# Two transformer blocks on one core: the front of the next block scaled inside its transposes, and four weight units of it split ahead into places of their own

## The chip, the core and the metric

The kernel runs on one core of a Trainium2 chip. The core has a matrix engine (TensorE, PE), a vector engine (VectorE, DVE), an activation engine (ScalarE, ACT), GpSimd (POOL) and SyncE (SP). Each has its own queue of instructions, and they wait for each other on semaphores. Data comes from HBM by DMA; here SP issues the loads of weights, POOL those of the conditioning matrix. The metric is device microseconds of one execution.

## What is computed

Two blocks on a sequence of 256 tokens with model width 2048, all in fp32:

```
def first_block(x, ...):
    h = rmsnorm(x, g_pre)
    o, z = swa_sink_mixer(h, w_in_a, sinks_a)
    y = (o * silu(z)) @ w_out_a
    return x + rmsnorm(y, g_post)

def second_block(x, c, ...):
    mod = silu(c) @ w_ada + b_ada
    sh1, sc1, gt1, sh2, sc2, gt2 = split(mod, 6)
    h = rmsnorm(x, g_pre_mix) * (1 + sc1) + sh1
    proj = h @ w_in
    ...                     # two attentions, gated, then @ w_o
    x = x + gt1 * rmsnorm(y, g_post_mix)
    h = rmsnorm(x, g_pre_ffn) * (1 + sc2) + sh2
    f = square(relu(h @ w_ff1)) @ w_ff2
    return x + gt2 * rmsnorm(f, g_post_ffn)
```

There are two places where a norm of a sum just made feeds the next product: `x` of the first block into `w_in` (called change 1), and `x` behind `w_o` into `w_ff1` (change 2).

## The kernel before

**Units and turns.** Weights go through the core in units of 128 x 1024 (two k tiles of 128 x 512, 512 KB). Eight units (`UPT`) are a turn: one product of all 16 k tiles with 512 columns of weights, for two tiles of 128 tokens. There are 76 turns. A unit is used in three fp32r products per k tile and token tile, `three` (L1751 to L1753): high part of h by high part of w, high by low, low by high; 12 products a unit. SP loads the unit into `raw` (4 slots), ACT rounds it into `w_hi` (L677), DVE subtracts into `w_lo` (L1109), both three units ahead of PE (`AHEAD`). A load waits for the low part of the unit four before, ACT's rounding for PE's products of the unit four before. The semaphores `hi_ready`, `lo_ready` and `mm_done` count these steps, and each engine does its steps in the order in which its function writes them; nothing else sets the order.

**The last turn before a change** (turn 12 before change 1, turn 43 before change 2) is `residual_turn`. PE does units 0 to 3 as usual, then units 4 to 7 for token tile 0 and only then for tile 1, so that the norm of tile 0 runs beside tile 1's products. DVE splits on to unit 7 (at change 1 with four products of conditioning, `ada_first`, between, and `make_mod`, which puts together the scale `pre_gain` and shift `pre_shift`, one column for each k tile). Behind the last products ACT squares the result (`square_y`), DVE scales it by the gain (`scale_y`) and adds it to x (`add_residual`, L1170), ACT squares x (`norm_squares`, L681) and takes roots, and DVE writes a diagonal matrix of 1/rms for each token tile (`diagonal_of`, L1210).

**The first turn behind it** (13 and 44) is `norm_turn`. PE transposes x, a k tile at a time (`norm_turned`, L1797), as soon as x is there, multiplies all ones by the diagonals into a bank, so that 1/rms stands in every row (L1826), and ACT copies that row (`norm_row`, L700). DVE then scales each transposed tile by gain and row (`norm_scale`, L1231), ACT adds the shift and rounds to `h_hi` (`norm_hi`, L707), DVE makes `h_lo` (`norm_lo`, L1238), two k tiles a unit. Unit 0 starts when the first k tile's `h_lo` is there (`front_unit`). Where PE has nothing to do it multiplies ones by the identity into an unused bank (`idle_at_change`, L1816), 12, 6 and 11 times (`IDLE_AT`).

**Conditioning.** The products of `silu(c)` with `w_ada` are done by DVE, one per 128 x 1024 (`ada_first`, L1114), between its other work; POOL loads their matrices into four buffers, each load behind the product that used the buffer before. `ADA_OUT` says at which units of turns 9 to 11 they stand. Later ones are for the gates and use two of the buffers.

## Time and profile before

| | |
|---|---|
| median of 3 runs | 1751.14 us (1750.18 to 1752.04) |
| profiled execution | 1750.48 us, its span 1748.8 us |
| PE busy with products | 1735.9 us, 99% of the span |
| DVE, ACT, POOL busy | 72%, 50%, 13% |
| DMA, mean | 264 GB/s |

The profile is of one execution. The page lists busy times, the chain of work that ended last and the costliest groups; the timeline lists instructions in order of time, counted from the span's start, and merges like ones that follow each other (x2). A record's time is from start to end, and records overlap in an engine's pipeline, so the step between starts can be less than the duration. An fp32 product that is no transpose shows as two records on PE. In brackets stands how long the engine was idle before, and what released it.

### The profile page before, as it was taken

To read this page: it belongs to the slowest core of one execution; us is meant where nothing else is said; L and a number is where in the kernel's file an instruction comes from. 1 tells how busy PE (TensorE), PEld (TensorE's weight loads), DVE (VectorE), ACT (ScalarE), POOL (GpSimd) and SP (SyncE) were. 2 spreads that over 40 slices of the span, in tenths; PEclk is the share of its full clock that TensorE was granted. 3 is DMA by queue.
4 is the path that set the end of the run, shared out by engine and by line. 5 is a ranking of instruction groups with operands and counts; after the bars stand their busy time and mean duration, and the time that the engine had idled before them with its cause. 6 is when DMAs were issued, how large, how long until landed. Compare 5 with 4: busy or idle time off the path is not lost.

```text
span 1748.8 us, 24683 instructions
## 1 busy us (share of the span) xinstructions
PE 1735.9 (99%) x8030; PEld 1433.7 (82%) x8030; DVE 1260.5 (72%) x1876; ACT 870.5 (50%) x1197; POOL 224.8 (13%) x446
## 2 busy tenths in 40 slices
PE   9999999999999999999999999999999999999998
PEld 7778878887888888888888888888888888888886
DVE  5798879868988788677678778777765555555555
ACT  6866674544445444444445455444444444444444
POOL 0232402001144233200001100000000000000000
PEclk9999999999999999999999999999999999999999
DMA  9899879554789888898998957999988765555553
GB/s 344 280 345 327 301 259 388 217 173 150 261 254 306 278 272 281 306 304 285 327 314 299 322 173 248 306 324 316 306 287 266 241 218 193 193 193 194 193 193 136
DMA packets 145663, 462.18 MB, mean 264 GB/s; under 512 B 21920, under 2 KB 33840, under 8 KB 144832
## 3 DMA queue, kind: packets, MB, share of 16 engines
q1 hardware_dynamic: 109200, 344.46, 58.6%
q0 software_dynamic: 36256, 116.91, 19.3%
q8 instruction: 33, 0.54, 0.1%
q14 instruction: 30, 0.25, 0.0%
q10 hardware_dynamic: 144, 0.02, 0.0%
HBM read 437.18 MB, written 12.08 MB: 257 GB/s over the span
## 4 chain that ended last, share of the span: by engine, by line
PE 94%; DVE 3%; ACT 2%; issue 1%; DMA 0%; SPq 0%; DVEq 0%; ACTq 0%
PE bank L1751 30%; PE bank L1752 30%; PE bank L1753 30%; PE bank L1788 1%; DVE w_lo L1109 0%; ACT w_hi L677 0%; PE bank L2028 0%; PE bank L2037 0%; DVE x L1170 0%; DMA raw<-in_w_in_a 0%; ACT y L681 0%; PE bank L1816 0%; PE bank L1906 0%; DVE ada_raw L1114 0%; DVE ada_more L1114 0%
## 5 line engine op out<-in xcount | busy, mean ns | idle before, releaser
L1109 DVE TENSOR_TENSOR w_lo<-raw,w_hi 128x1024 fp32r<-128x1024 f32 x605 | 728.5, 1210 | 433.3 <-ACT w_hi L677 429.2
L677 ACT ACTIVATE w_hi<-raw 128x1024 fp32r<-128x1024 f32 x605 | 633.8, 1050 | 736.8 <-PE bank L1753 666.2
L1751 PE MATMUL bank<-w_hi,h_hi 128*128 128x512 f32 x2272 | 889.5, 391 | 2.7 <-DVE w_lo L1253 1.2
L1752 PE MATMUL bank<-w_lo,h_hi 128*128 128x512 f32 x2272 | 884.3, 389 | 0.0
L1753 PE MATMUL bank<-w_hi,h_lo 128*128 128x512 f32 x2272 | 884.3, 389 | 0.0
L1751 PEld LDWEIGHTS bank<-w_hi,h_hi 128*128 128x128 f32 x2272 | 426.5, 188 | 96.3 <-issue 6.4
L1753 PEld LDWEIGHTS bank<-w_hi,h_lo 128*128 128x128 f32 x2272 | 426.4, 188 | 89.2
L1752 PEld LDWEIGHTS bank<-w_lo,h_hi 128*128 128x128 f32 x2272 | 426.6, 188 | 86.7
L1114 DVE CUSTOM_DVE_ANT_0 ada_raw<-ada_raw,cond 128x1024 f32<-128x1024 f32 x160 | 194.5, 1217 | 9.2 <-DMA ada_raw<-in_w_ada 9.2
L549 POOL DMA_DIRECT2D ada_raw<-in_w_ada x160 | 85.4, 534 | 784.8 <-DVE loop_sums L1114 586.4
L402 POOL DMA_DIRECT2D rope_ab<-rot x96 | 47.1, 499 | 142.7 <-DVE rot L1454 141.9
L405 POOL DMA_DIRECT2D p_back<-post_gain x100 | 49.0, 499 | 32.8 <-ACT post_gain L827 20.6
L1751 PE MATMUL bank<-w_hi,o_hi 128*128 128x512 f32 x128 | 49.8, 389 | 0.0
L1752 PE MATMUL bank<-w_lo,o_hi 128*128 128x512 f32 x128 | 49.8, 389 | 0.0
L1753 PE MATMUL bank<-w_hi,o_lo 128*128 128x512 f32 x128 | 49.8, 389 | 0.0
L1114 DVE CUSTOM_DVE_ANT_0 ada_more<-ada_more,cond 128x1024 f32<-128x1024 f32 x32 | 38.5, 1218 | 0.0
L1751 PEld LDWEIGHTS bank<-w_hi,o_hi 128*128 128x128 f32 x128 | 24.0, 188 | 5.0
L1063 ACT ACTIVATE f_buf<-bank 128x512 f32<-128x512 f32 x32 | 19.2, 600 | 17.9 <-PE bank L1753 17.9
L1752 PEld LDWEIGHTS bank<-w_lo,o_hi 128*128 128x128 f32 x128 | 24.0, 188 | 5.0
L1753 PEld LDWEIGHTS bank<-w_hi,o_lo 128*128 128x128 f32 x128 | 24.0, 188 | 5.0
L549 POOL DMA_DIRECT2D ada_more<-in_w_ada x32 | 17.0, 531 | 54.6 <-DVE loop_sums L1114 24.1
L1691 DVE STREAM_TRANSPOSE f_buf<-f_buf 128x512 f32<-128x512 f32 x32 | 22.8, 711 | 1.1
(240 smaller groups left out, 867.4 us busy)
## 6 DMA issues: line engine op xcount, KB each, us to landing
raw<-in_w_ff SPq DMA_DIRECT2D x256, 512.0 KB, 4.6
raw<-in_w_in SPq DMA_DIRECT2D x176, 512.0 KB, 5.0
ada_raw<-in_w_ada POOLq DMA_DIRECT2D x160, 512.0 KB, 6.2
raw<-in_w_in_a SPq DMA_DIRECT2D x69, 512.0 KB, 6.2
ada_more<-in_w_ada POOLq DMA_DIRECT2D x32, 512.0 KB, 6.2
raw<-in_w_out_a SPq DMA_DIRECT2D x32, 512.0 KB, 6.5
raw<-in_w_o SPq DMA_DIRECT2D x32, 512.0 KB, 5.2
raw<-in_w_moba SPq DMA_DIRECT2D x16, 512.0 KB, 5.6
```

Of the source, the lines that this page charges most:

```text
L402: eng.dma_start(rope_ab[j * QUAD:(j + 1) * QUAD, i * T * P:(i + 1) * T * P], rot_flat[i * QUAD:(i + 1) * QUAD, j * T * P:(j + 1) * T * P]) ...
L405: eng.dma_start(back[j * QUAD:(j + 1) * QUAD, i * MASK_W:(i + 1) * MASK_W], blocks[i * QUAD:(i + 1) * QUAD, j * MASK_W:(j + 1) * MASK_W]). ...
L549: pool.dma_start(two(ada_slot(slot), 1), w_ad[:, bass.ds((k + part * KT) * 2 + half, 1), :])\
L677: act.activation(used(w_hi, turn, s), used(raw, turn, s), ACT.Copy).then_inc(hi_ready, 1)
L1063: act.activation(f_tok[:, t, :], pair[p][t][:, :], ACT.Relu).then_inc(evicted[p][t], 1)
L1109: dve.tensor_tensor(used(w_lo, turn, s), used(raw, turn, s), used(w_hi, turn, s).bitcast(F32), ALU.subtract).then_inc(lo_ready, 1)
L1114: dve.tensor_tensor_reduce(w, w, cond[:, half * (D // 2):(half + 1) * (D // 2)], 1.0, 0.0, ALU.mult, ALU.add, dst).then_inc(ada_done, 1)
L1691: dve.transpose(by_quadrant[:, t], f_tok[:, t, :]).then_inc(f_blocked, 1)
L1751: pe.matmul(out_ap, hi, rhs_hi, start=start, stop=False)
L1752: pe.matmul(out_ap, hi, rhs_lo, start=False, stop=False)
L1753: return pe.matmul(out_ap, lo, rhs_hi, start=False, stop=stop)
L1788: ins = pe.transpose(dst[:, b * P:(b + 1) * P], src[:, t, b * P:(b + 1) * P], ident)
```

## The change

The first two k tiles are no longer transposed and then scaled. PE multiplies them by the diagonal of 1/rms (`front_turn`), which turns and scales in one, into two banks of their own (`front_bank`); ACT applies `pre_gain` and `pre_shift` and rounds straight from the bank (`front_hi`), and DVE makes the low part in two steps, bank times gain minus high, then plus shift (`front_lo`). The row of 1/rms is still made for the other k tiles. PE's fill products go from 12, 6 and 11 to 12, 4 and none.

Units 0 to 3 of the turn behind the change get buffers of their own (`ext_raw`, `ext_hi`, `ext_lo`, the low part over the raw one), loaded, rounded and subtracted in the last turn before the change, each behind a unit of that turn. Units 4 to 7 are loaded into the usual slots and split in the turn itself (`NEXT_SPLITS`). The four conditioning products that stood in turn 12 stand now at units 0 to 3 of turn 9, and the others keep their units. Space for that comes from moving the scratch `sq1`, `sq2` into `f_buf`. The diff, without the buffers' places and the counts of semaphores:

```diff
...
+        sq1 = sq2 = f_buf[:, 3 * CH:4 * CH]
...
-        ADA_OUT = (range(4, 8), range(0, 8), range(0, 8))
+        ADA_OUT = (range(0, 8), range(0, 8), range(0, 8))
...
-        IDLE_AT = (12, 6, 11)
+        IDLE_AT = (12, 4)
+        def front_bank(k):
+            return pair[PAIR_B][1] if k else banks[SCORES]
...
+        NEXT_SPLITS = {0: 4, 1: 5, 2: 6, 3: 7, 5: 8, 6: 9, 7: 10}
...
+            def load_ext(r, s, src):
+                if s == 0 and r == 1:
+                    sp.wait_ge(og_ready, T * (CHUNKS + 1))
+                if s == 0 and r == 2:
+                    sp.wait_ge(mm_done, TURN_WO * UPT)
+                    sp.wait_ge(h_lo_ready, H_WO + UPT)
+                sp.dma_start(two(ext_raw[r][:, s, :], 1), src).then_inc(ext_loaded[s], 16)
+            def load_last(r, turn, w, c, w_next, c_next):
+                for s in range(UPT):
+                    load(turn, s, unit_at(w, c, s))
+                    if s < EXT:
+                        load_ext(r, s, unit_at(w_next, c_next, s))
+                for s in range(EXT, UPT):
+                    load(turn + 1, s, unit_at(w_next, c_next, s))
...
-            with sp.Fori(0, CHUNKS) as i:
+            with sp.Fori(0, CHUNKS - 1) as i:
                 load_chunk(i + TURN_OUT, w_oa, i)
-            load_chunk(TURN_QI, w_2, CHUNK_QI)
+            load_last(1, TURN_QI - 1, w_oa, CHUNKS - 1, w_2, CHUNK_QI)
...
-            with sp.Fori(0, D // CH) as i:
+            with sp.Fori(0, D // CH - 1) as i:
                 load_chunk(i + TURN_WO, w_oo, i)
+            load_last(2, TURN_FF1 - 1, w_oo, CHUNKS - 1, w_f1, 0)
...
                 pool.dma_start(x[:, t, :], x_in[t * P:(t + 1) * P, :]).then_inc(x_again, 16)
+            for n in range(UPT // 2):
+                load_first(40, n, SC1, 14)
             pool.wait_ge(o1_ready, (CHUNKS - 1) * PAIRS_A + 2)
             load_gain(0, g_post)
-            for n in range(UPT // 2):
-                load_first(40, n, SC1, 14)
             for n in range(2 * UPT):
...
                 act.activation(used(w_hi, turn, s), used(raw, turn, s), ACT.Copy).then_inc(hi_ready, 1)
+            def split_ext(r, turn, s):
+                act.wait_ge(ext_loaded[s], 16 * r)
+                if s == 0 and r == 1:
+                    act.wait_ge(h_lo_ready, H_OUT + UPT)
+                if s == 0 and r == 2:
+                    act.wait_ge(mm_done, TURN_WO * UPT)
+                act.activation(ext_hi[r][:, s, :], ext_raw[r][:, s, :], ACT.Copy).then_inc(hi_ready, 1)
+            def split_next(turn, s):
+                act.wait_ge(raw_loaded[s % SLOTS], (turn * (UPT // SLOTS) + s // SLOTS + 1) * 16)
+                act.wait_ge(mm_done, unit_of(turn - 1, s) + 1)
+                act.activation(used(w_hi, turn, s), used(raw, turn, s), ACT.Copy).then_inc(hi_ready, 1)
...
+            def front_hi(r):
+                act.wait_ge(mod_ready, r)
+                for k in range(KG):
+                    act.wait_ge(front_turned, KG * (r - 1) + k + 1)
+                    act.activation(h_hi[:, k, :], front_bank(k)[:, 0:SEQ], ACT.Identity, bias=pre_shift[:, k:k + 1],
+                                   scale=pre_gain[:, k:k + 1]).then_inc(n_rounded, 1)
...
             def norm_turn(r, turn):
-                for s in range(2):
-                    norm_hi(r, s)
-                split(turn, 2)
-                for s in range(UPT):
-                    split(turn, s + AHEAD)
+                norm_hi(r, 1)
+                for s in range(UPT):
+                    if s in NEXT_SPLITS:
+                        (split_next if s < EXT else split)(turn, NEXT_SPLITS[s])
                     if s + 2 < UPT:
...
                     split(turn, s + AHEAD)
+                    if s:
+                        act.sem_inc(raw_loaded[s - 1], 16)
+                    if s < EXT:
+                        split_ext(r, turn, s)
                 for t in range(T):
...
                     y_roots(r, t, n + t + 1)
-                    if t == 0:
-                        split(turn, UPT)
-                    else:
+                    if t:
                         front_root(r)
-                        split(turn, UPT + 1)
                     norm_squares(r, t, y)
                 back_root(r)
+                front_hi(r)
                 norm_row(r)
...
                                   ALU.subtract).then_inc(lo_ready, 1)
+            def split_last(turn, s):
+                dve.wait_ge(hi_ready, count_last(turn, s))
+                dve.tensor_tensor(w_lo[:, s % SLOTS, :], raw[:, s % SLOTS, :], w_hi[:, s % SLOTS, :].bitcast(F32),
+                                  ALU.subtract).then_inc(lo_ready, 1)
+            def split_ext(r, turn, s):
+                dve.wait_ge(hi_ready, count_ext(turn, s))
+                dve.tensor_tensor(ext_lo[r][:, s, :], ext_raw[r][:, s, :], ext_hi[r][:, s, :].bitcast(F32),
+                                  ALU.subtract).then_inc(lo_ready, 1)
...
                 for s in range(TILE_FROM + 1):
-                    split(turn, s + AHEAD)
-                    if r == 1 and s < TILE_FROM:
-                        ada_first(60, s, mod_column(SC1, s // 2, s % 2))
+                    split_last(turn, s + AHEAD)
+                    if s < EXT:
+                        split_ext(r, turn, s)
                     if s == TILE_FROM - 1:
...
                     add_residual(r, t, y)
-                    if t == 0:
-                        split(turn, UPT)
                 back_stats(r)
-                split(turn, UPT + 1)
                 dve.wait_ge(mod_ready, r)
                 norm_first(r, pre_gain)
-                split(turn, UPT + 2)
...
+            def front_lo(r, gain):
+                for k in range(KG):
+                    rest = norm_tmp[:, 0, k * SEQ:(k + 1) * SEQ]
+                    dve.wait_ge(n_rounded, KT * r + k + 1)
+                    dve.scalar_tensor_tensor(rest, front_bank(k)[:, 0:SEQ], gain[:, k:k + 1], h_hi[:, k, :].bitcast(F32),
+                                             ALU.mult, ALU.subtract).then_inc(n_scaled, 1)
+                    dve.wait_ge(n_scaled, KT * (r - 1) + k + 1)
+                    dve.tensor_scalar(h_lo[:, k, :], rest, pre_shift[:, k:k + 1], None, ALU.add)\
+                        .then_inc(h_lo_ready if k else h_front_ready, 1)
...
             def norm_first(r, gain):
-                norm_scale(r, 0, gain)
-                norm_lo(r, 0)
+                front_lo(r, gain)
                 norm_scale(r, 1, gain)
...
                 for s in range(UPT):
-                    split(turn, s + AHEAD)
+                    if s in NEXT_SPLITS:
+                        split(turn, NEXT_SPLITS[s])
                     if s + 2 < UPT:
...
+            def ext_unit(r, turn, s, p, h):
+                pe.wait_ge(h_lo_ready, h + s + 1)
+                pe.wait_ge(lo_ready, count_ext(turn - 1, s))
+                for t in range(T):
+                    mm = unit_tile(s, t, h_hi, h_lo, KG * s, p, False, False, w_at=(ext_hi[r][:, s, :], ext_lo[r][:, s, :]))
+                mm.then_inc(mm_done, 1)
+            def front_turn(r, t, k):
+                pe.wait_ge(x_stat, X_STATS[r] + (8 if t else 4))
+                pe.wait_ge(x_new, ((r - 1) * T + t) * CHUNKS + 1)
+                return pe.matmul(front_bank(k)[:, t * P:(t + 1) * P], x[:, t, k * P:(k + 1) * P], rstd_diag[:, t, :],
+                                 start=True, stop=True)
             def idle_at_change(r, n):
...
                 idle_at_change(r, IDLE_AT[0])
-                for s in range(ahead):
+                for s in range(1, ahead):
                     norm_turned(r, s)
                 idle_at_change(r, IDLE_AT[1])
-                pe.wait_ge(x_stat, X_STATS[r] + 7)
+                for k in range(KG):
+                    front_turn(r, 0, k)
+                for k in range(KG):
+                    front_turn(r, 1, k).then_inc(front_turned, 1)
                 for t in range(T):
...
                 ins.then_inc(rstd_spread, 1)
-                idle_at_change(r, IDLE_AT[2])
-                for s in range(UPT):
-                    if s:
+                for s in range(UPT):
+                    if s == 0:
+                        front_unit(r, turn, p, use, h)
+                    elif s < EXT:
+                        ext_unit(r, turn, s, p, h)
+                    else:
                         chunk_unit(turn, s, p, use, h)
-                    else:
-                        front_unit(r, turn, p, use, h)
                     if s in (0, 2):
...
                             norm_turned(r, turned)
```

On PE, from the last product of turn 12 to unit 0 of turn 13 (`consts` holds ones and identity, `norm_rows` the diagonals). Before:

```order
L1753 MATMUL bank<-w_hi,h_lo 128x512
L1816 MATMUL bank<-consts 128x128 x12
L1797 MATMUL bank<-consts,x 128x128 x16
L1816 MATMUL bank<-consts 128x128 x6
L1826 MATMUL bank<-norm_rows,consts 128x128 x2
L1816 MATMUL bank<-consts 128x128 x11
L1751 MATMUL bank<-w_hi,h_hi 128x512
```

The same place after:

```order
L1819 MATMUL bank<-w_hi,h_lo 128x512
L1894 MATMUL bank<-consts 128x128 x12
L1864 MATMUL bank<-consts,x 128x128 x12
L1894 MATMUL bank<-consts 128x128 x4
L1890 MATMUL bank<-norm_rows,x 128x128 x4
L1907 MATMUL bank<-norm_rows,consts 128x128 x2
L1817 MATMUL bank<-ext_hi,h_hi 128x512
```

Four transposes have become four products with the diagonals, ahead of the spreading of the row, and nothing stands between that and unit 0 any more.

On DVE, from tile 1's root to the low parts of unit 1 (`post_gain` holds the scaled tiles). Before:

```order
L1208 RECIPROCAL x_rstd<-x_rstd 128x1
L1210 TENSOR_SCALAR norm_rows<-consts,x_rstd 128x128
L1109 TENSOR_TENSOR w_lo<-raw,w_hi 128x1024
L1231 SCALAR_TENSOR_TENSOR post_gain<-bank,pre_gain,norm_rows 128x256 x2
L1238 SCALAR_TENSOR_TENSOR h_lo<-post_gain,pre_shift,h_hi 128x256 x2
L1231 SCALAR_TENSOR_TENSOR post_gain<-bank,pre_gain,norm_rows 128x256 x2
```

The same place after:

```order
L1265 RECIPROCAL x_rstd<-x_rstd 128x1
L1267 TENSOR_SCALAR norm_rows<-consts,x_rstd 128x128
L1302 SCALAR_TENSOR_TENSOR post_gain<-bank,pre_gain,h_hi 128x256
L1305 TENSOR_SCALAR h_lo<-post_gain,pre_shift 128x256
L1302 SCALAR_TENSOR_TENSOR post_gain<-bank,pre_gain,h_hi 128x256
L1305 TENSOR_SCALAR h_lo<-post_gain,pre_shift 128x256
L1288 SCALAR_TENSOR_TENSOR post_gain<-bank,pre_gain,norm_rows 128x256 x2
```

The split of a weight unit is gone from there, and the front's k tiles take turns instead of going in pairs.

On DVE in turn 12, from unit 6's low part to unit 7's (the five short ones are `make_mod`). Before, with a product of conditioning behind unit 6:

```order
L1109 TENSOR_TENSOR w_lo<-raw,w_hi 128x1024
L1114 ISA ada_more,mod_part<-ada_more,cond 128x1024
L1114 ISA mod_part 128x1
L1130 TENSOR_TENSOR pre_gain<-mod_part 128x16
L1132 TENSOR_TENSOR pre_gain<-pre_gain,mods 128x16
```

The same place after:

```order
L1166 TENSOR_TENSOR w_lo<-raw,w_hi 128x1024
L1170 TENSOR_TENSOR ext_lo<-ext_raw,ext_hi 128x1024
L1191 TENSOR_TENSOR pre_gain<-mod_part 128x16
L1193 TENSOR_TENSOR pre_gain<-pre_gain,mods 128x16
```

An early split of the next turn's unit stands where the product stood; so it is behind units 3, 4 and 5 too.

## Rows read from the trace of the kernel before

**Rows 1.** The page, the chain that ended last, by line of the kernel.
```profile
PE bank L1751 30%; PE bank L1752 30%; PE bank L1753 30%; PE bank L1788 1%; DVE w_lo L1109 0%; ACT w_hi L677 0%; PE bank L2028 0%; PE bank L2037 0%; DVE x L1170 0%; DMA raw<-in_w_in_a 0%; ACT y L681 0%; PE bank L1816 0%; PE bank L1906 0%; DVE ada_raw L1114 0%; DVE ada_more L1114 0%
```

**Rows 2.** Timeline, change 1: start us, us, engine, line, operation [idle before].
```profile
330.49 0.39 PE L1753 MATMUL bank<-w_hi,h_lo 128*128 128x512 f32 x1
...
333.35 0.63 ACT L681 ACTIVATE y<-x 128x512 f32<-128x512 f32 x1 [0.32 <-DVE x L1170]
...
336.48 0.16 DVE L1208 RECIPROCAL x_rstd<-x_rstd 128x1 f32<-128x1 f32 x1 [0.53 <-ACT x_rstd L696]
...
336.67 0.29 DVE L1210 TENSOR_SCALAR norm_rows<-consts,x_rstd 128x128 f32<-128x128 f32 x1
...
337.01 0.71 PE L1826 MATMUL bank<-norm_rows,consts 128*128 128x128 f32 x4 [0.34 <-DVE norm_rows L1210]
...
337.56 2.62 PE L1816 MATMUL bank<-consts 128*128 128x128 f32 x22
...
337.76 0.38 ACT L700 ACTIVATE norm_rows<-bank 128x256 f32<-128x256 f32 x1 [1.32 <-PE bank L1826]
...
338.28 0.88 DVE L1231 SCALAR_TENSOR_TENSOR post_gain<-bank,pre_gain,norm_rows 128x256 f32<-128x256 f32 x2 [0.18 <-ACT norm_rows L700]
...
338.86 0.91 ACT L707 ACTIVATE h_hi<-post_gain,pre_shift 128x256 fp32r<-128x256 f32 x2 [0.71 <-DVE post_gain L1231]
...
339.40 0.89 DVE L1238 SCALAR_TENSOR_TENSOR h_lo<-post_gain,pre_shift,h_hi 128x256 fp32r<-128x256 f32 x2 [0.24 <-ACT h_hi L707]
...
340.03 0.47 PE L1751 MATMUL bank<-w_hi,h_hi 128*128 128x512 f32 x1
```

**Rows 3.** Timeline, change 2: last product before it, first behind it.
```profile
1032.84 0.39 PE L1753 MATMUL bank<-w_hi,h_lo 128*128 128x512 f32 x1
...
1042.44 0.47 PE L1751 MATMUL bank<-w_hi,h_hi 128*128 128x512 f32 x1
```

**Rows 4.** Groups by line and shape: count, busy us, mean ns, idle before.
```profile
L1529 DVE TENSOR_SCALAR post_gain<-s,l_inv 128x256 f32<-128x256 f32 x16 | 5.6, 348 | 0.0
```

**Rows 5.** Windows: us, PE, PEld, DVE, ACT, POOL busy, PEclk, DMA share, GB/s.
```profile
248.00:259.00 11.00, 11.00 (x64) 8.45 (x63) 5.58 (x10) 6.72 (x12) 0.00 (x0) 1.00 0.44 147
...
292.00:303.00 11.00, 11.00 (x50) 9.13 (x49) 9.90 (x13) 4.25 (x4) 2.61 (x5) 1.00 1.02 412
...
340.00:351.00 11.00, 11.00 (x58) 9.28 (x57) 10.81 (x21) 8.28 (x13) 0.00 (x0) 1.00 0.38 129
```

**Rows 6.** Timeline, turn 9: DVE's gating and low parts, PE's unit 6.
```profile
257.03 1.29 DVE L1344 TENSOR_TENSOR o_gated_t<-bank,o_t 128x512 f32<-128x512 f32 x2 [1.01 <-PE bank L1788]
...
259.02 1.30 DVE L1275 TENSOR_TENSOR h_lo<-o_gated_t,h_hi 128x512 fp32r<-128x512 f32 x2 [0.70 <-ACT h_hi L763]
...
259.97 0.39 PE L1751 MATMUL bank<-w_hi,h_hi 128*128 128x512 f32 x1
```

**Rows 7.** DMA issues, that of 292.98 alone: KB, us to landing.
```profile
raw<-in_w_out_a SPq DMA_DIRECT2D x1, 512.0 KB, 6.7
```

**Rows 8.** Timeline, end of turn 12: DVE, then PE's first product of unit 7.
```profile
318.47 1.23 DVE L1109 TENSOR_TENSOR w_lo<-raw,w_hi 128x1024 fp32r<-128x1024 f32 x1 [0.35 <-ACT w_hi L677]
...
319.61 1.22 DVE L1114 CUSTOM_DVE_ANT_0 ada_more<-ada_more,cond 128x1024 f32<-128x1024 f32 x1
...
320.94 0.17 DVE L1130 TENSOR_TENSOR pre_gain<-mod_part 128x16 f32<-128x16 f32 x1
...
321.75 1.22 DVE L1109 TENSOR_TENSOR w_lo<-raw,w_hi 128x1024 fp32r<-128x1024 f32 x1
...
323.92 0.39 PE L1751 MATMUL bank<-w_hi,h_hi 128*128 128x512 f32 x1
```

**Rows 9.** Windows, columns as in rows 5: loads ahead of change 2.
```profile
1000.00:1011.00 11.00, 11.00 (x50) 9.13 (x49) 8.50 (x11) 4.93 (x6) 1.58 (x3) 1.00 0.89 298
```

**Rows 10.** Timeline at the start; a window behind the last product.
```profile
1.21 4.90 PE L1840 MATMUL bank<-s 128*128 128x128 f32 x22 [1.21 <-POOL s L581]
...
1743.30:1748.00 4.70, 0.00 (x0) 0.00 (x0) 2.52 (x4) 0.00 (x0) 0.00 (x0) 0.50 0.62 223
```

59 lines of the change are left out of this document (38 added, 21 removed).

## Prediction

> **What bounds the kernel now.** I read the page first: TensorE (PE) carries 94% of the chain that ended last, and 90% of the span are the products of weight units, three lines of 30% each [rows 1]. So the time changes only where PE stands still, does work that is no product, or would come to stand still. The changed code touches two stretches, the changes between blocks, so I read the timeline there. At change 1 the last product before it starts at 330.49 and the first after it at 340.03 [rows 2]; at change 2 these are 1032.84 and 1042.44 [rows 3]. In between PE does transposes and products of constants that nobody reads. What really ends the stretch is a chain through four engines: square of the last result, scaling by the gain, square root, four residual additions, their squares, a root, the diagonal of 1/rms written by VectorE (DVE) at 336.67 for 0.29 us; then PE spreads it over all rows (337.01), ScalarE (ACT) copies the row (337.76), DVE scales the transposed tiles (338.28), ACT rounds and shifts (338.86), DVE makes the low part (339.40), PE begins (340.03) [rows 2]. From the diagonal's arrival on PE to the first product that is 3.02 us. Change 2 shows the same durations 702.4 us later [rows 3], so what is worked out for one counts twice.
>
> **Part 1, the shorter chain (a gain).** Everything up to 337.01 stays: the same operations in the same order; the splits of weights taken out there (one on ACT, one on DVE) stood beside waits: ACT sat idle for 0.32 us before its squares of the second half, until DVE's addition released them [rows 2]. After 337.01 the row copy and one DVE pass go. New chain: two PE records per fp32 product. The first of a batch takes 0.38 and four take 0.71 with steps of 0.11 behind the first step [rows 2], so two take 0.71-0.22 = 0.49. Then ACT, scaling and shifting out of the bank: between 0.38, its copy out of a bank of the same size [rows 2], and 0.50, its shift of 128x256 (two in 0.91, 0.41 apart); I take 0.50, since scale and shift are the latter's kind. DVE's product-minus-high from the bank: 0.48 (two in 0.88, 0.40 apart) [rows 2]. DVE's add of the shift, 128x256 from SBUF: between 0.35, a tensor_scalar of that size [rows 4], and the same 0.48; I take 0.35. Hops between steps are 0.03 (DVE to itself, 336.64 to 336.67), 0.05 (DVE to PE, 336.96 to 337.01) and 0.14 (ACT to DVE, 338.14 to 338.28) [rows 2]; I take 0.2 for all four. Sum 0.49+0.50+0.48+0.35+0.2 = 2.02; against 3.02 that gains 1.0. With 0.48 for the add and hops of 0.15 it is 2.45, a gain of 0.55. I take 0.95 per change, 1.9 in all.
>
> The second half of the first unit waits for the other tile's low part. On DVE that is 0.48+0.35 plus hops behind the first, 0.9 us, while PE has 6 products of 0.23 = 1.4 us to do, so it costs nothing. Unit 1 then needs scaling, rounding and low part of its two tiles; for unit 0 these took 338.28 to 340.29, 2.0 us [rows 2]. From DVE's end with the front at 339.8 that gives 341.8, while PE has unit 0 (12 products, 2.7 us) and eight transposes (1.0 us) to do from 339.1 and comes at 342.8. Nothing is late behind.
>
> **Part 2, four units split ahead.** In the stretch behind the change PE had no gap to give back, busy 11.00 of 11 us, with DVE at 10.81 and ACT at 8.28 [rows 5]. So early splits gain nothing there. Their work is the same count of splits (1.06 on ACT, 1.22 on DVE, where the next starts after 1.14 [rows 8]) moved into the last turn before a change, where PE takes 2.72 per unit and the two splits need 2.1 and 2.3: they fit if data is there. The four conditioning products (1.22 each) that stood there at change 1 go to the start of turn 9.
>
> **Part 3, their new place (nothing, up to 1).** In turn 9 they stand with the attention of the last heads. DVE is busy only 5.58 of 11 us at 248 to 259 [rows 5]. In its order the last of the four stands ahead of a split of weights that ended 1.0 us before the gating which reads PE's transposes (idle 1.01, start 257.03) [rows 6]. One product of 1.14 us (DVE's step) more ahead of it makes the gating 0.1 late; the other three stand further ahead, in idle time. Behind it hangs the low part of the unit that PE begins at 259.97; it is ready at 259.02+0.65 = 259.67 [rows 6]. 0.3 us of slack takes that. I count 0; if the products fall badly, up to one of them, 1.2.
>
> **Part 4, the transfers (a cost at change 1).** SP now issues an extra 512 KB behind each of the first four loads of turn 12, issued at 293 to 301. There the DMA engines are already full, at 412 GB/s and a share of 1.02 [rows 5], and a load lands 6.7 us after its issue [rows 7]. At 0.412 MB/us one load of 0.524 MB takes 1.27 us alone and 2.53 beside POOL's. Unit 0 of turn 12 lands at 299.7 (issued 292.98). Up to unit 4 there now come 8 loads instead of 4. POOL's last conditioning load is issued where DVE's fourth product of turn 11 ends, at about 299.4, and lands at about 307; until then 7.3/2.53 = 2.9 loads get through; the other 5.1 take 6.5 us, to 313.5. The four loads that POOL issued behind it are gone, but its next two, for the gate, wait only for the count of finished products, which is now reached at about 308 and 312; they take about one load's time from SP's queue, 1.4 us. So unit 4 lands at about 314.9. From there ACT and DVE have a full row: high part 1.06, six low parts at steps of 1.14 (units 4 to 6 and three extras), the modulation vectors 0.81 (320.94 to 321.75) and the low part of unit 7, 1.22: 9.96 with the hop, done at 324.9. PE begins the products of unit 7 at 323.92, and had its low part at 322.97 [rows 8]. That is a stall of 1.0 us, and each us of the landing is one of the stall. The bounds: all eight loads at the full rate, 299.7+10.2 = 309.9, no stall; all at half, 299.7+20.2 = 319.9, a stall of 6.0.
>
> Those two rates are the row's total and its half. On who gets which share the Trainium skill (DMA: Bandwidth & Descriptors, Queues, rings and completion order) says that an engine takes turns between the queues that have work, packet by packet. By that rule SP's queue has half as long as POOL's has work, and the stall stays at about 1.0; were SP's queue served first it would be none.
>
> At change 2 the same extra loads meet less, 298 GB/s [rows 9]. Four of them in about 9 us add 0.23 MB/us, which makes 0.53 against 0.412, 1 MB too much by their end or 2.5 us of delay. Change 1 had 1.0 us between low part and need although its loads landed 2 us later after issue, so I count 0, at most 0.5.
>
> **Sum.** Against the profiled execution: -1.9 for the two chains, +1.0 for the late unit at change 1: -0.9, 1750.48 to 1749.6. That execution lies 0.7 under the median of the runs shown, so against it 1751.14-0.9 = 1750.2.
>
> **Rivals.** (a) No stall: the queue drains in time. For it: only 1 us separates landing and need. Time 1751.14-1.9 = 1749.2. (b) The extra loads stay at half rate, because POOL's gate loads come early and the products' loads stretch: PE stands up to 6.0 us at unit 7 of turn 12. This alone ends slower than before: it does from a landing of unit 4 at 315.9 on, and at 319.9 gives 1751.14-1.9+6.0 = 1755.2. Against it: POOL's queue is empty for some time after 307. (c) The clock. PE loses 13 of 29 fill products per change, and stands still some 0.5 us before the diagonal and 0.6 us before the first product. The trace shows 22 records of 128x128 in 4.90 us at the start [rows 10] against 22 in 2.62 us at change 1 [rows 2]: the lower level (1.2 GHz) at first, 2.4 GHz later; the granted clock is 1.00 in every window of the changes [rows 5] and 0.50 only behind the last product, where PE does nothing [rows 10]. If each change brings the lower level for as long as the start had it, 4.9 us, half is lost: 2.4 per change, 1751.14-1.9+4.8 = 1754.0. The rows speak against it: the new order stands still for less than 1 us at a time, and only behind the last product has standing still cost the level.
>
> The Trainium skill (TensorE: Matmul & The Clock Gate, What's actually happening) has the gate follow how busy PE was lately, which speaks against removing fill work; how much is enough no row here shows, so (c) keeps a small chance.
>
> (d) The chain is not shortened at all, because something beside it is late (a turned tile, a bank): 0 or a little more, 1751.1 to 1752. (e) More than both chains comes back; nothing in the rows offers it.
>
> **Chances.** Forecast (stall 0.2 to 2.0) 43%; (a) 30%; (b) beyond 2.0 10%; (c) 5%; (d) 6%; (e) 6%. About 0.2% (3.5 us, 1747.6 to 1754.6) is what a measurement of this kernel can tell from no change. Faster than that: (e) and 2% of (a), 8%. Slower: the far part of (b), and (c) where it comes with the stall, 8%. The rest, 84%, is within. The range: the low end is (a) with both gains at 1.0 and the spread of the runs, 1751.14-2.0-1.0 = 1748.1; the high end takes in (d) and most of (b), 1753.0.
>
> **What would show it.** The first product after change 1 should start about 2.0 us after PE's product with the diagonal starts, and likewise at change 2. Loads of units 1 to 4 of turn 12 should take 9 to 11 us to land instead of 7; DVE's low part of unit 7 should end about 1 us later against PE's products, with a gap on PE before the products of that unit. The clock row should stay at 1.00. The forecast is wrong if the chain from diagonal to product is above 2.5 us, or if PE shows gaps of more than 2 us anywhere in turns 9 to 12.

## The result, and the profile after

| | before | after |
|---|---|---|
| median of 20 runs | 1750.84 us (1749.90 to 1752.04) | 1753.53 us (1750.35 to 1755.56) |
| profiled execution | 1750.48 us, span 1748.8 | 1751.51 us, span 1749.8 |

The ratio is 1.0014, interval 1.0008 to 1.0020: 2.7 us slower, where the prediction had 1750.2 and a range up to 1753.0. The runs after also scatter more, 5.2 us from lowest to highest instead of 2.1, and the profiled execution is one of the quick ones. So one trace can't hold the whole answer.

PE after the change, from the late part of turn 12 to the first product behind change 1 (columns as in rows 2):

```profile
323.06 0.50 PE L1817 MATMUL bank<-w_hi,h_hi 128*128 128x512 f32 x1 [0.61 <-DVE w_lo L1166]
...
324.32 0.40 PE L1819 MATMUL bank<-w_hi,h_lo 128*128 128x512 f32 x1
326.14 0.50 PE L1817 MATMUL bank<-w_hi,h_hi 128*128 128x512 f32 x1 [1.42 <-DVE w_lo L1166]
326.48 0.39 PE L1818 MATMUL bank<-w_lo,h_hi 128*128 128x512 f32 x1
...
332.85 0.39 PE L1819 MATMUL bank<-w_hi,h_lo 128*128 128x512 f32 x1
333.08 2.84 PE L1894 MATMUL bank<-consts 128*128 128x128 f32 x24
335.75 1.73 PE L1864 MATMUL bank<-consts,x 128*128 128x128 f32 x12
337.32 1.06 PE L1894 MATMUL bank<-consts 128*128 128x128 f32 x8
338.21 0.61 PE L1890 MATMUL bank<-norm_rows,x 128*128 128x128 f32 x4
339.38 0.71 PE L1890 MATMUL bank<-norm_rows,x 128*128 128x128 f32 x4 [0.55 <-DVE norm_rows L1267]
339.92 0.61 PE L1907 MATMUL bank<-norm_rows,consts 128*128 128x128 f32 x4
341.65 0.47 PE L1817 MATMUL bank<-ext_hi,h_hi 128*128 128x512 f32 x1 [1.12 <-DVE h_lo L1305]
```

Against [rows 2], the last product to the first behind it is 332.85 to 341.65, 8.80 us instead of 9.54. The gain of the chain is there. But ahead of it stand two new waits, 0.61 before unit 6 and 1.42 before unit 7 of turn 12, where PE ran through before. Each costs some 0.3 us more than the idle time in brackets: products start 0.23 apart when nothing holds them up, but from 324.32 to 326.14 it is 1.82, and 0.34 more to the next.

What those waits hang on is the row of splits on DVE; the same trace:

```profile
315.62 1.22 DVE L1170 TENSOR_TENSOR ext_lo<-ext_raw,ext_hi 128x1024 fp32r<-128x1024 f32 x1
317.25 1.23 DVE L1166 TENSOR_TENSOR w_lo<-raw,w_hi 128x1024 fp32r<-128x1024 f32 x1 [0.41 <-ACT w_hi L714]
...
321.80 1.22 DVE L1166 TENSOR_TENSOR w_lo<-raw,w_hi 128x1024 fp32r<-128x1024 f32 x1
322.93 1.22 DVE L1170 TENSOR_TENSOR ext_lo<-ext_raw,ext_hi 128x1024 fp32r<-128x1024 f32 x1
324.07 0.17 DVE L1191 TENSOR_TENSOR pre_gain<-mod_part 128x16 f32<-128x16 f32 x1
...
324.87 1.22 DVE L1166 TENSOR_TENSOR w_lo<-raw,w_hi 128x1024 fp32r<-128x1024 f32 x1
```

From unit 4 (317.25) to unit 7 (its low part ends at 326.09) DVE never waits for data. It started late because ACT did, and ACT waited for the load of unit 4:

```profile
316.15 1.06 ACT L714 ACTIVATE w_hi<-raw 128x1024 fp32r<-128x1024 f32 x1 [1.67 <-DMA raw<-in_w_out_a]
```

That load was issued at 303.09 and took 13.0 us to land; before, unit 4's took 7.0, and that of unit 0, in [rows 7], 6.7:

```profile
raw<-in_w_out_a SPq DMA_DIRECT2D x1, 512.0 KB, 13.0
```

The windows (columns as in rows 5) show where the DMA engines' time was full: from 292 to 314 the share is 1.00 and 1.03, and the window behind that, with 0.65, is the first in which PE is not busy all the time.

```profile
292.00:303.00 11.00, 11.00 (x51) 9.09 (x50) 10.38 (x14) 4.25 (x4) 2.65 (x5) 1.00 1.00 399
303.00:314.00 11.00, 11.00 (x50) 9.13 (x49) 6.66 (x11) 4.92 (x8) 0.86 (x2) 1.00 1.03 412
314.00:325.00 11.00, 10.11 (x44) 7.59 (x42) 10.49 (x15) 7.23 (x8) 0.20 (x1) 1.00 0.65 242
```

The kernel before had the same full engines up to 314, with nothing late, so a full share alone doesn't tell of a stall; its windows from 303 on:

```profile
303.00:314.00 11.00, 11.00 (x50) 9.09 (x50) 10.30 (x15) 5.52 (x8) 2.12 (x4) 1.00 1.03 415
314.00:325.00 11.00, 11.00 (x50) 9.13 (x49) 8.82 (x19) 3.18 (x3) 1.06 (x2) 1.00 0.90 312
```

**Cutting the span.** Since executions scatter by more than the effects, I cut each trace at five starts on PE: the first product of probabilities with values in turn 4 (L1906 before, L1988 after), the first fill behind turn 12, the first product behind change 1, the first fill and the first product at change 2; "rest" ends where PE's last product starts. "Change 1" and "change 2" in the table are the stretches from first fill to first product. Such a stretch repeats to about 0.1 us when nothing disturbs it. The start of the kernel does not: the first cut lies anywhere from 100.33 to 103.26 in these traces, with code there that is the same.

| kernel | first cut | to change 1 | change 1 | to change 2 | change 2 | rest | this execution |
|---|---|---|---|---|---|---|---|
| before | 101.01 | 229.71 | 9.31 | 693.04 | 9.37 | 698.03 | 1750.48 |
| after | 100.68 | 232.40 | 8.57 | 693.25 | 8.62 | 698.00 | 1751.51 |

So the change costs 2.69 ahead of change 1, and gains 0.74 and 0.75 at the two changes; the start was 0.33 earlier by chance. That explains 1751.5, but not the median of 1753.5, 1.3 above what these parts give (1750.84+2.69-1.49+0.2 = 1752.2).

### The profile page after: what moved, and what is told of

Read it like the earlier page. It is cut to its first block, busy times and chain, and to the rows that moved or that the text cites. A ratio compares the mean times of both kernels' runs of the same rounds, so it can differ in the third digit from the quotient of the medians.

```text
span 1749.8 us, 24558 instructions
## 1 busy us (share of the span) xinstructions
PE 1732.1 (99%) x7986; PEld 1428.9 (82%) x7986; DVE 1260.5 (72%) x1876; ACT 869.4 (50%) x1197; POOL 225.5 (13%) x446
## 4 chain that ended last, share of the span: by engine, by line
PE 92%; DVE 3%; ACT 2%; DMA 1%; issue 1%; SPq 0%; DVEq 0%; ACTq 0%
PE bank L1817 30%; PE bank L1819 29%; PE bank L1818 29%; DMA raw<-in_w_out_a 1%; ACT w_hi L714 1%; PE bank L1855 1%; DVE w_lo L1162 1%; PE bank L2110 0%; PE bank L2119 0%; DVE x L1231 0%; ACT y L729 0%; DMA raw<-in_w_in_a 0%; PE bank L1988 0%; DVE ada_raw L1175 0%; DVE ada_more L1175 0%
## 5 line engine op out<-in xcount | busy, mean ns | idle before, releaser
L1162 DVE TENSOR_TENSOR w_lo<-raw,w_hi 128x1024 fp32r<-128x1024 f32 (+1 forms) x587 | 707.0, 1210 | 430.0 <-ACT w_hi L714 426.1
L714 ACT ACTIVATE w_hi<-raw 128x1024 fp32r<-128x1024 f32 x589 | 617.2, 1050 | 732.9 <-PE bank L1819 638.8
L1817 PE MATMUL bank<-w_hi,h_hi 128*128 128x512 f32 x2240 | 876.9, 391 | 4.9 <-DVE w_lo L1166 2.0
L1818 PE MATMUL bank<-w_lo,h_hi 128*128 128x512 f32 x2240 | 871.9, 389 | 0.0
L1819 PE MATMUL bank<-w_hi,h_lo 128*128 128x512 f32 x2240 | 871.8, 389 | 0.0
L1817 PEld LDWEIGHTS bank<-w_hi,h_hi 128*128 128x128 f32 x2240 | 420.6, 188 | 97.5 <-issue 6.2
L1819 PEld LDWEIGHTS bank<-w_hi,h_lo 128*128 128x128 f32 x2240 | 420.5, 188 | 88.0
L1818 PEld LDWEIGHTS bank<-w_lo,h_hi 128*128 128x128 f32 x2240 | 420.7, 188 | 85.8
```

Source lines behind the costliest of these rows:

```text
L714: act.activation(used(w_hi, turn, s), used(raw, turn, s), ACT.Copy).then_inc(hi_ready, 1)
L1162: dve.tensor_tensor(used(w_lo, turn, s), used(raw, turn, s), used(w_hi, turn, s).bitcast(F32), ALU.subtract).then_inc(lo_ready, 1)
L1817: pe.matmul(out_ap, hi, rhs_hi, start=start, stop=False)
L1818: pe.matmul(out_ap, hi, rhs_lo, start=False, stop=False)
L1819: return pe.matmul(out_ap, lo, rhs_hi, start=False, stop=stop)
```

## The experiments

All are timed beside runs of the kernel before. The intervals of a ratio with 11 runs are 0.0009 to either side, or 1.6 us, so the medians alone settle few of the questions. The stretches of the table tell more, but each is of one profiled execution.

### Taking the change apart

**chain_only**: the kernel before with the scaled transposes alone.

```diff
-                norm_scale(r, 0, gain)
-                norm_lo(r, 0)
+                front_lo(r, gain)
...
-                for s in range(2):
-                    norm_hi(r, s)
+                norm_hi(r, 1)
...
                 back_root(r)
+                front_hi(r)
                 norm_row(r)
...
-        IDLE_AT = (12, 6, 11)
+        IDLE_AT = (12, 4)
```

> The kernel before with Part 1 alone: the front scaled inside its transposes, all splits, loads and conditioning where they were. Theory (transfers): the extra time of the changed kernel comes from its loads in turn 12, none from the new chain; its profile gives 2.27 us from PE's product with the second diagonal to the first product instead of 3.02, so each change should gain 0.75 us and the time fall by 1.5, from 1750.8 to 1749.3, with runs as close together as those of the kernel before (some 2 us from lowest to highest). Rival (chain): the new order on PE and ACT is what costs or scatters; then this kernel is at 1751 or above, and its runs spread over 4 us or more.

Measured 1749.59 (1749.07 to 1752.90) beside 1750.92; ratio 0.9993, 0.9984 to 1.0002. To change 1 it takes 229.75, as before, and the changes 8.57 and 8.63. Nine runs lie within 1 us, two at 1752.80 and 1752.90. The second is the profiled one, and it has a late start (103.26) and a wait of 1.11 us just before 948, for DVE's `y_tok`, far from what was changed; the clock is at 1.00. The first has a mean granted clock of 0.997, the lowest of the eleven, as a fall of the clock would leave it; the others have 0.998 and 0.999. So the median is as the theory had it and the scatter is not. The gain of the chain is seen in the stretches and is all there without the rest; the interval of the ratio alone still holds 1.

**ext_only**: the changed kernel with the old chain.

```diff
-                front_lo(r, gain)
+                norm_scale(r, 0, gain)
+                norm_lo(r, 0)
...
-        IDLE_AT = (12, 4)
+        IDLE_AT = (12, 6, 11)
```

> The changed kernel with the old chain put back: the early splits, their loads and the move of the conditioning products stay. Theory (transfers): PE again stands before units 6 and 7 of turn 12, 2 us in a good run and more in others; without the 1.5 us of the two chains the median is 1753.5+1.5 = 1755.0, and the runs spread over 4 us or more. Rival (chain): 1750.8 to 1751.5, close together.

Measured 1754.10 (1752.08 to 1754.79); ratio 1.0017, 1.0008 to 1.0026. Gaps of 0.60 and 1.41 before units 6 and 7, 232.77 to change 1, and 9.31 and 9.37 at the changes. The early splits with their loads cost 3.1 us, all of it ahead of change 1.

**cond_only**: the kernel before with the four conditioning products moved to turn 9.

```diff
-        ADA_OUT = (range(4, 8), range(0, 8), range(0, 8))
+        ADA_OUT = (range(0, 8), range(0, 8), range(0, 8))
...
-                    if r == 1 and s < TILE_FROM:
-                        ada_first(60, s, mod_column(SC1, s // 2, s % 2))
```

> The kernel before with only the four conditioning products moved from turn 12 to turn 9. Theory (transfers): nothing, 1750.8 within 0.4; in the changed kernel the trace shows no gap of PE in turn 9. Rival (conditioning): the products hold up the gating of turn 9 or their loads push those of weights, by up to 1.2 us in one run and more in others; then 1752 or above.

Measured 1750.95 (1750.14 to 1752.13); ratio 0.9999, 0.9990 to 1.0008. Behind the start, all stretches are as before to 0.04 us, 229.71 to change 1 among them. The move costs nothing.

### Work or transfers

**thin_ext**: hardly any bytes, same splits. The extra loads bring 16 of 1024 columns, the early splits read the unit before (so the product behind each change is another), and the load of unit 7 waits for one more low part, since that slot is now read once more.

```diff
-                sp.dma_start(two(ext_raw[r][:, s, :], 1), src).then_inc(ext_loaded[s], 16)
+                sp.dma_start(two(ext_raw[r][:, s, 0:16], 1), src[:, :, 0:16]).then_inc(ext_loaded[s], 16)
...
+                    if s == UPT - 1:
+                        sp.wait_ge(lo_ready, unit_of(turn, s) - SLOTS + 2)
...
-                act.activation(ext_hi[r][:, s, :], ext_raw[r][:, s, :], ACT.Copy).then_inc(hi_ready, 1)
+                act.activation(ext_hi[r][:, s, :], raw[:, (s + AHEAD) % SLOTS, :], ACT.Copy).then_inc(hi_ready, 1)
```

> The changed kernel with the extra loads cut to 16 of their 1024 columns. The early splits stay, on ACT and DVE, in their places and of full size, but they read the unit split just before, so what the next turn multiplies by is not its weights. Theory (transfers): 4 MB less go through the queues ahead of the changes, the gaps of turn 12 go, and the time is 1749.4, as with the shorter chains alone. Rival (work): the extra split of each engine per unit is what makes unit 6 and 7 late; then the gaps stay and the time is 1752 or more.

229.69 to change 1, with no gap of PE in turn 12. So the stall is the loads' alone, and the splits fit into turn 12, as the prediction had it. But the median was 1750.72 (1748.75 to 1754.06) instead of 1749.4, and the profile shows one reason. PE behind change 1 in thin_ext:

```profile
339.62 0.72 PE L1819 MATMUL bank<-ext_hi,h_hi 128*128 128x512 f32 x1 [1.12 <-DVE h_lo L1307]
340.14 0.63 PE L1820 MATMUL bank<-ext_lo,h_hi 128*128 128x512 f32 x1
340.57 0.63 PE L1821 MATMUL bank<-ext_hi,h_lo 128*128 128x512 f32 x1
...
343.11 0.39 PE L1821 MATMUL bank<-ext_hi,h_lo 128*128 128x512 f32 x1
```

Its window there, with the granted clock in the third column from the end:

```profile
339.00:343.00 4.00, 3.38 (x8) 2.74 (x9) 3.75 (x11) 2.54 (x6) 0.00 (x0) 0.58 0.00 0
```

The products step by 0.43 us, not 0.23, for 3.4 us: the lower level of 1.2 GHz, and 1.6 us lost (694.80 to change 2 instead of 693.2). It came with the first product, behind 0.55 and 1.12 us of standing still. This is rival (c), which had 5%.

**late_ext**: the extra loads in the order in which the units are split.

```diff
                     load(turn, s, unit_at(w, c, s))
-                    if s < EXT:
-                        load_ext(r, s, unit_at(w_next, c_next, s))
+                    if s >= AHEAD and s < AHEAD + EXT:
+                        load_ext(r, s - AHEAD, unit_at(w_next, c_next, s - AHEAD))
```

> The changed kernel with another order of SP's loads alone: each extra load stands three places later, behind units 3 to 6 of the last turn, in the order in which the units are split. Theory (transfers): five loads fewer stand ahead of what is wanted first, unit 4 lands before 312 instead of at 316.1, the gaps before units 6 and 7 go, and the time is that of the shorter chains alone, 1749.3, runs within 2 us. Rival (work): in turn 12 ACT and DVE have an extra split per unit and can't keep up whatever the loads do; then the gaps stay, and the time is 1753 as for the changed kernel.

Measured 1751.76 (1749.77 to 1753.81), between the 1749.3 and the 1753 of the two theories; ratio 1.0005, 0.9996 to 1.0014. Unit 4 lands at 313.17, and it takes 231.26 to change 1: 1.1 us less than in the changed kernel's profile, but not all of the stall. One gap of 1.22 is left before unit 7. What ends last there is the last extra unit, which lands at 322.10; ACT waits for it, and the low part of unit 7 stands behind its low part and the modulation vectors in DVE's order:

```profile
322.12 1.06 ACT L721 ACTIVATE ext_hi<-ext_raw 128x1024 fp32r<-128x1024 f32 x1 [0.19 <-DMA ext_raw<-in_w_in]
...
323.21 1.23 DVE L1170 TENSOR_TENSOR ext_lo<-ext_raw,ext_hi 128x1024 fp32r<-128x1024 f32 x1
```

The bytes are the same, and moving them back only moves what is late.

**gate_late**: POOL's two gate loads held back.

```diff
+            pool.wait_ge(mm_done, TURN_QI * UPT)
             for n in range(2):
                 load_gate(ADA_FIRST, n, 0)
```

> The changed kernel with POOL's two loads for the gate, issued at 309.6 and 313.7 in turn 12, held back until the last product of turn 12; they are not needed before turn 16. Theory (transfers, all streams count alike): 1 MB less competes with units 4 to 7, which land 1.3 to 2.5 us earlier; 2.7 us of loss in turns 9 to 12 become 0.2 to 1.4, and the time falls to between 1750.5 and 1752.0. Rival (backlog from turn 11): only what is issued before 301 counts, and the time stays at 1753.

Measured 1752.83 (1751.41 to 1754.76); ratio 1.0011, 1.0002 to 1.0020. The 1750.5 to 1752.0 expected is missed. The gaps are 0.61 and 1.42 as ever, and it takes 232.68. Units 4 to 7 do land quicker (12.0, 8.2, 5.3 and 3.1 us after issue instead of 13.0, 9.3, 7.5 and 5.6), but DVE was busy without a break from unit 2 on, and unit 2 had waited for its load, issued before any gate load:

```profile
311.33 1.06 ACT L715 ACTIVATE w_hi<-raw 128x1024 fp32r<-128x1024 f32 x1 [3.10 <-DMA raw<-in_w_out_a]
```

In the changed kernel's profile DVE's break before unit 4 is 0.41 us, so that is about all that an earlier landing of unit 4 alone can give (an estimate): the landing of unit 2 binds next, and the gate loads come too late to touch it. The landing of unit 4 here:

```profile
raw<-in_w_out_a SPq DMA_DIRECT2D x1, 512.0 KB, 12.0
```

This trace also has a gap of 1.07 before unit 7 of turn 43, and 694.63 to change 2: the stall that the prediction excluded at change 2.

**late_both**: the two edits above together.

> Both remedies in one: the extra loads three places later in SP's queue, and POOL's two gate loads held back until the end of turn 12. The first alone left 1.55 us of loss up to the last product of turn 12 and a time of 1751.8. Theory (transfers, all streams count alike): 1 MB less is worth 1.3 to 2.5 us of landing, the rest of the stall goes, and the time is that of the shorter chains alone, 1749.4. Rival (work): what is left in turn 12 is the extra splits; the time stays at 1751.8.

229.73 to change 1: the stall is gone, and the same edits with fill (late_both_fill below) have 229.75. The two together did what neither did alone: with the extra loads further back, the loads that come last are those beside which the gate loads ran. Median 1750.23 (1748.86 to 1752.16); ratio 0.9996, 0.9987 to 1.0005. Unit 4 landed in

```profile
raw<-in_w_out_a SPq DMA_DIRECT2D x1, 512.0 KB, 7.8
```

Its profiled execution, 1752.16, had the clock at 0.50 for 3.4 us behind change 2 (699.59 in the rest instead of 698.0).

### What the slower runs lose

**after2**: the changed kernel once more.

> The changed kernel once more, beside the others of this group. In its profile so far PE stood 0.61 and 1.42 us before units 6 and 7 of turn 12, and from the first mixing products of turn 4 to the last product of turn 12 it took 2.7 us more than before; the two shorter chains give back 1.5, which makes 1.2 over the kernel before, or 1752.1. Its median was 1753.5. Theory (transfers): most runs have a longer stall than the profiled one, so a second profile may show more than 2.0 us of gaps there. Rival: the rest lies elsewhere, and the gaps of turn 12 are as they were.

Median 1753.43 (1750.78 to 1754.86), ratio 1.0011, 1.0002 to 1.0021; again a quick execution was profiled, with 232.46 to change 1, gaps of 0.62 and 1.41, and nothing else. The gaps are as they were; whether the slower runs have a longer stall stays open here.

**after_fill**: fill products in both gaps of each change. chain_fill, late_both_fill, late2_fill and thin_fill have the same edit.

```diff
-        IDLE_AT = (12, 4)
+        IDLE_AT = (12, 4, 2, 4)
...
+            def fill_at_front(p, use, n):
+                pe.wait_ge(evicted[p][1], use)
+                for _ in range(n):
+                    pe.matmul(pair[p][1][:, 0:P], ones, ident, start=True, stop=True)
...
                 for k in range(KG):
                     front_turn(r, 0, k)
+                fill_at_front(p, use, IDLE_AT[2])
                 for k in range(KG):
                     front_turn(r, 1, k).then_inc(front_turned, 1)
...
                 ins.then_inc(rstd_spread, 1)
+                fill_at_front(p, use, IDLE_AT[3])
```

> The changed kernel with six fill products back at each change, where PE stood still: two before the products with the second diagonal (a gap of 0.55 us) and four before the first weight product (a gap of 1.12 us), at 0.24 us each. One profile of a related kernel showed the granted clock at 0.50 for 3.4 us from the first product behind change 1 on, and one behind change 2; that costs 1.6 us each time. Theory (clock): most runs of the changed kernel lose the clock at one of the changes, which is the 1.3 us that its median of 1753.4 lies above what its profiled runs explain (1752.1); with the fill it is at 1752.1, and the clock stays at 1.00. Rival (stall at change 2): fill changes nothing, 1753.4.

> The shorter chain alone, which was at 1749.6 with 2 of 11 runs at 1752.8, with the same six fill products at each change. Theory (clock): where PE stands still for 0.55 and 1.12 us the clock may fall; with the fill no run does it, the median is 1749.4 and no run lies above 1751.5. Rival: the two runs at 1752.8 come from the start of the kernel and a gap of 1.1 us at 947 as the profiled one did; then some of these lie at 1752.8 too, and the median is the same.

> The changed kernel with all remedies: extra loads three places later, gate loads held back, six fill products at each change. Without the fill it was at 1750.2, and its profiled run lost 1.6 us at change 2 with the clock. Theory (clock): 1749.5, as the shorter chain alone, and the clock stays at 1.00. Rival: 1750.2 as before, the rest being a stall that comes in some runs.

| | without fill | with fill |
|---|---|---|
| changed kernel | 1753.43 (1750.78 to 1754.86) | 1752.44 (1750.94 to 1753.14) |
| chain alone | 1749.59 (1749.07 to 1752.90) | 1749.78 (1748.62 to 1751.12) |
| late_both | 1750.23 (1748.86 to 1752.16) | 1749.55 (1748.19 to 1750.93) |

The highest run falls in all three. But the two columns come from different sessions, beside medians of the kernel before of 1750.92 to 1751.05, and each difference lies within the interval of 1.6 us; the kernel before itself had single runs up to 1755.35. So the table points to the clock and doesn't show it. PE at change 1 in chain_fill; the first product still starts 2.28 us behind the product with the second diagonal, so the fill delays nothing:

```profile
335.62 0.61 PE L1838 MATMUL bank<-consts 128*128 128x128 f32 x4
336.34 0.71 PE L1830 MATMUL bank<-norm_rows,x 128*128 128x128 f32 x4
336.89 0.61 PE L1852 MATMUL bank<-norm_rows,consts 128*128 128x128 f32 x4
337.34 1.06 PE L1838 MATMUL bank<-consts 128*128 128x128 f32 x8
338.62 0.47 PE L1764 MATMUL bank<-w_hi,h_hi 128*128 128x512 f32 x1 [0.22 <-DVE h_lo L1255]
```

late_both_fill is the best version that keeps the early splits: ratio 0.9989, 0.9980 to 0.9998. chain_fill, without any of them, stands at 0.9992, 0.9983 to 1.0001, so the early splits themselves show no gain.

**late2**: the extra loads three places later at change 2 alone.

```diff
-                    if s < EXT:
-                        load_ext(r, s, unit_at(w_next, c_next, s))
+                    n = s - AHEAD if r == 2 else s
+                    if 0 <= n < EXT:
+                        load_ext(r, n, unit_at(w_next, c_next, n))
```

> The changed kernel with the extra loads three places later at change 2 alone (behind units 3 to 6 of turn 43); at change 1 they stay. The profile of the kernel without gate loads in turn 12 showed a gap of 1.07 us before unit 7 of turn 43, which the profiles of the changed kernel itself didn't show; with the slow products around it turn 43 took 1.4 us more. Theory (stall at change 2): most runs of the changed kernel have it, so here the median falls from 1753.4 to 1752.1. Rival (clock): no change, 1753.4.

Measured 1752.61 (1751.32 to 1754.10); ratio 1.0007, 0.9998 to 1.0016. This is between the 1752.1 and the 1753.4 expected and decides nothing. Its profile shows 234.11 to change 1, with four waits before units of turn 12 that sum to 3.0 us: the stall of turn 12 itself varies from run to run.

```profile
PE bank L1818 <- DVE w_lo L1167: 3.0, 4, 1.4
```

**after_look1, 2 and 3**: three more executions of the changed kernel.

> The changed kernel, one profiled execution, in search of one above 1753. It has run at 1753.4 to 1753.5 in the median and so far was profiled only at 1751.5 and 1751.8, where up to the last product of turn 12 it lost 2.7 us and nothing at change 2 or by the clock. Theory (clock): an execution above 1753 shows the granted clock at 0.50 for 3.4 us behind a change, worth 1.6. Theory (stall): it shows more than 3 us of loss in turns 9 to 12, or 1.4 in turn 43, with the clock at 1.00.

> As the one before: the changed kernel, one more profiled execution. Above 1753 the clock theory wants 3.4 us at the lower level behind a change, the stall theory more than 3 us lost in turns 9 to 12 or some in turn 43.

> As the two before: the changed kernel, one more profiled execution, read in the same way.

| kernel | first cut | to change 1 | change 1 | to change 2 | change 2 | rest | this execution |
|---|---|---|---|---|---|---|---|
| after2 | 100.95 | 232.46 | 8.58 | 693.24 | 8.62 | 698.03 | 1751.83 |
| look 1 | 101.25 | 231.88 | 8.58 | 695.32 | 8.62 | 699.61 | 1755.19 |
| look 2 | 102.50 | 232.93 | 8.57 | 693.39 | 8.62 | 698.00 | 1753.95 |
| look 3 | 101.59 | 232.76 | 8.57 | 693.27 | 8.63 | 697.98 | 1752.78 |

Look 1 has everything at once: 2.2 lost in turn 12, 2.1 in turn 43, 1.6 by the clock behind change 2. PE in turn 43:

```profile
1030.06 0.50 PE L1817 MATMUL bank<-w_hi,h_hi 128*128 128x512 f32 x1 [1.41 <-DVE w_lo L1166]
```

Here the load of unit 4 of turn 43 took 12.5 us to land:

```profile
raw<-in_w_o SPq DMA_DIRECT2D x1, 512.0 KB, 12.5
```

In gate_late, the other trace with a stall there, it took 11.7; in the six that have these loads in their place and no stall, 8.3 to 9.7. So it is a stall of the same kind as in turn 12. The windows of look 1 around the fall of the clock (0.50 in the middle one, with PE busy throughout):

```profile
1043.00:1046.00 3.00, 1.51 (x10) 1.30 (x11) 1.59 (x5) 1.29 (x3) 0.00 (x0) 0.99 0.00 0
1046.00:1049.30 3.30, 3.30 (x9) 2.61 (x8) 3.11 (x8) 2.59 (x5) 0.00 (x0) 0.50 0.00 0
1049.30:1052.00 2.70, 2.70 (x17) 2.27 (x16) 2.70 (x6) 1.85 (x4) 0.00 (x0) 0.99 0.33 94
```

Look 2, with the clock at 1.00, shows that a late start and a longer stall do as much without it. So both theories hold, each for some runs.

**late2_fill**: both remedies.

> The changed kernel with the six fill products at each change and the extra loads three places later at change 2 alone. With the fill alone it was at 1752.4, with the later loads alone at 1752.6. If both the clock and a stall at change 2 cost something, this one is at 1751.8 or below, and what is left over the shorter chains (1749.5) is the stall of turn 12 alone, 2.3 to 2.7; if the two remedies hit the same cause, it stays at 1752.4.

Measured 1752.21 (1751.17 to 1754.81); ratio 1.0009, 0.9999 to 1.0018. That is between the two expectations and can't tell them apart; its profile had 233.44 to change 1, and 694.36 to change 2, 1.1 more than most, with small waits at 542 and before unit 7 of turn 43 (1031), where the later loads had been meant to help.

**thin_fill**: no extra bytes, and fill.

> The changed kernel with the extra loads cut to 16 of 1024 columns (the early splits read the unit before, so the product behind each change is not the reference's) and six fill products at each change. Without the fill it was at 1750.7, with turn 12 back at its old length and, in its profile, 3.4 us at the lower clock behind change 1. If the loads make the stalls and the missing fill the falls of the clock, both are gone: 1749.5, no run above 1751.5, clock at 1.00. If something else of the early splits costs, it stays at 1750.7.

Measured 1749.48, all 11 runs within 1749.07 and 1750.17; ratio 0.9992, 0.9983 to 1.0001. With loads and clock out of the way nothing of the change's cost is left, and the scatter is smaller than that of the kernel before. It is 1.2 us faster than the kernel before beside it; the two chains give 1.5 in the stretches.

**before_bare**: the kernel before without the last fill.

```diff
-        IDLE_AT = (12, 6, 11)
+        IDLE_AT = (12, 6, 0)
```

> The kernel before, without the 11 fill products ahead of the first weight product of each change; PE stands still for 2.3 us there. If standing still at a change is what lets the clock fall, some or all executions lose 1.6 us at a change, the median is 1751 to 1754, and the profile may show the granted clock at 0.50 for 3.4 us from the first product on. If the falls belong to the new order alone, it stays at 1750.9.

Measured 1754.43 (1751.27 to 1756.61) beside 1750.71; ratio 1.0021, 1.0012 to 1.0030. Removing 22 products that nobody reads costs 3.7 us. The mean granted clock, on record for every run, shows that the profiled one is no exception: 0.996 or 0.997 in nine of the eleven and 0.998 in the two quickest, against 0.998 and 0.999 in the 21 runs beside them. A fall for 3.4 us takes 0.001 off such a mean, so two falls were the rule. Its PE at change 1:

```profile
337.66 0.71 PE L1826 MATMUL bank<-norm_rows,consts 128*128 128x128 f32 x4 [0.34 <-DVE norm_rows L1210]
340.68 0.47 PE L1751 MATMUL bank<-w_hi,h_hi 128*128 128x512 f32 x1 [2.30 <-DVE h_lo L1238]
340.98 0.40 PE L1752 MATMUL bank<-w_lo,h_hi 128*128 128x512 f32 x1
341.22 0.48 PE L1753 MATMUL bank<-w_hi,h_lo 128*128 128x512 f32 x1
341.50 0.63 PE L1751 MATMUL bank<-w_hi,h_hi 128*128 128x512 f32 x1
```

The windows behind both changes (granted clock third from the end):

```profile
341.00:345.00 4.00, 4.00 (x12) 3.14 (x11) 3.81 (x8) 3.60 (x6) 0.00 (x0) 0.57 0.10 40
...
1044.30:1048.30 4.00, 3.67 (x9) 2.95 (x10) 3.81 (x9) 3.05 (x6) 0.00 (x0) 0.57 0.26 100
```

The stretches behind the two changes are 694.59 and 699.55, 1.5 longer each. The fall belongs to standing still and not to the new order. The Trainium skill (TensorE: Matmul & The Clock Gate, What's actually happening) has the gate go by how busy PE was lately; the rows agree: with the fill gone PE did less there, and the level fell.

## Why the prediction was wrong, point by point

**What bounds the kernel: right.** All that was found to move the time was PE standing still, or PE at half its clock.

**Part 1, the chain: right, the size a little off.** From PE's product with the second diagonal (339.38) to the first product (341.65) are 2.27 us, where the sum had 2.02 and the slow variant 2.45. In this trace ACT starts 0.58 behind PE (the sum: 0.49 and a hop), takes half of its 1.02 for the first tile, DVE follows 0.16 later with 0.48 and 0.35:

```profile
339.96 1.02 ACT L753 ACTIVATE h_hi<-bank,pre_shift,pre_gain 128x256 fp32r<-128x256 f32 x2 [1.16 <-PE bank L1890]
340.63 0.48 DVE L1302 SCALAR_TENSOR_TENSOR post_gain<-bank,pre_gain,h_hi 128x256 f32<-128x256 f32 x1 [1.31 <-ACT h_hi L753]
...
341.15 0.35 DVE L1305 TENSOR_SCALAR h_lo<-post_gain,pre_shift 128x256 fp32r<-128x256 f32 x1
```

The durations were right to 0.02; the term that was short is the hops, 0.2 for all, where they sum to 0.4 (0.09, 0.16, 0.04 and 0.15). Gain 0.75 per change instead of 0.95, shown in every kernel with the new chain (8.57 against 9.31).

**Part 2 and Part 3, early splits and conditioning: right.** thin_fill and cond_only show nothing for either. The stretch behind change 1 even grew by 0.2, all of it a wait at about 433 that is 0.37 to 0.41 in the kernels with the new chain instead of 0.18; its cause stays open. With 8.57 in every new chain, rival (d) is out, and no run shows anything of rival (e).

**Part 4, change 1: mechanism right, the landing mis-sized.** This is the largest miss of the sum: +1.0 was forecast, and five profiles of the changed kernel lost 2.8 in the mean. The step that failed is "unit 4 lands at about 314.9": it landed at 316.13, which is 316.5 on the clock of the trace before, since this one started 0.33 earlier. The row from landing to the low part of unit 7 took 9.96 us, as summed. So 1.6 us more of landing made 1.0 of stall into the 2.7 measured. Units 1 to 4 took 10.4, 12.2, 12.1 and 13.0 us to land, where 9 to 11 had been expected. Two terms of the landing were short, both on the clock of the trace before: unit 0 landed at 300.3 instead of 299.7, and the last of POOL's conditioning loads at 309.0 instead of 307, so the half rate lasted longer. Put into the prediction's own sum, the two give 316.2 (an estimate); the remaining 0.3 stays open. The sum also let the full row begin with unit 4, while in gate_late and look 1 it is full from unit 2 on. The size varies by run: ten profiles with the extra loads in their place at change 1 lost 2.2 to 4.4 us, 3.1 in the mean. Rival (b), "beyond 2.0", had 10% and was the rule.

**Part 4, change 2: wrong.** "I count 0, at most 0.5." Eight profiles have the extra loads of change 2 in their place; six show nothing, two lose 1.4 and 2.1. The prediction had itself worked out 2.5 us of delay there, and set against it the slack and the landing of one execution at change 1; landing is what varies between executions (8.3 to 12.5 us for unit 4 of turn 43).

**Rival (c), the clock: wrong in its chance.** It was priced from the start of the kernel at 2.4 per change; a fall costs 1.6. It was argued away with "the new order stands still for less than 1 us at a time" (the trace has 1.12) and "only behind the last product has standing still cost the level", which was so because the fill was there. Eleven profiles of the new chain without the added fill show 3 falls in 22 changes; five with it, none in 10; before_bare 2 in 2. The first two counts may differ by chance; that standing still brings the fall is shown by before_bare. At 0.27 falls a run that is 0.4 us in the mean, and 1.6 in a run with one. The mean granted clock of the runs agrees that falls are rare in the changed kernel: 0.9985 over the eleven runs of after2, 0.9986 over the 33 of the kernel before beside them, in steps of 0.001 for each run. In thin_ext it is 0.9981, with fill 0.9989.

**The sum.** The terms, from profiles: turn 12 +2.8 (mean of the five of the changed kernel), chains -1.5, behind change 1 +0.2, turn 43 +0.4, clock +0.4: +2.3, against 2.7 measured. The missing 0.4 may lie in the start of the kernel or in what few profiles can give as a mean; no run decides it. That the stall of turn 12, that of turn 43 and the fall of the clock occur is shown; how often each does is only estimated from few executions.

**The range** was too narrow because it was built from one execution's slack. A stall that hangs on a queue should have had its spread on the upper side.

## What to carry to other kernels

Before adding loads to a stretch, look at the DMA share of the stretch and of the one ahead of it: where it is already 1, every extra load was paid in landing time by the loads behind it, and holding back loads that come later than the first late unit didn't help by itself. Products that nobody reads may carry the clock: when a change takes fill away because the chain got shorter, fill what is left of the gap, after checking that the fill ends before the next step is released. And when runs scatter more than the effect, cut the traces at fixed instructions and compare stretches, and profile more than one execution before calling a slack safe.

## What the runs showed of the hardware that I had not expected

- With PE standing still for 0.34 and 2.30 us shortly one after the other, the granted clock fell to 0.50 within 0.7 us of the first product and for 3.4 us, at both changes of the profiled execution of before_bare; with 0.55 and 1.12 us it fell at 3 of 22 changes. Each fall cost 1.5 to 1.6 us.
- The same start of the kernel reached its first cut between 100.33 and 103.26 us in different traces. This alone is a scatter as large as all effects here.
- While POOL's and SP's queues both had work, SP's 512 KB loads landed 2.5 us apart (305.86, 308.40 in the changed kernel's trace), and 1.28 apart (312.45, 313.73) when SP's was alone: the two shared about evenly, as the prediction took it.
